# Sums of squares of the gated DeltaNet's queries and keys: two products in fp32r in place of one in float32

## The reference, cut to what matters

```python
def l2norm(x):
    return x * lax.rsqrt(jnp.sum(x * x, -1, keepdims=True) + L2_EPS)

    q = l2norm(c[..., :W_DN].reshape(B, T, H_DN, HEAD_DIM)) * HEAD_DIM ** -0.5
    k = l2norm(c[..., W_DN:2 * W_DN].reshape(B, T, H_DN, HEAD_DIM))
```

## Time and profile before

| | |
|---|---|
| median of three runs | 1552.3 us |
| the profiled execution's own time | 1559.0 us |
| its span | 1557.2 us |
| granted TensorE clock, mean | 0.992 of 2.4 GHz |
| PE busy | 1508.7 us |
| VectorE (DVE) busy | 912.4 us |
| ScalarE (ACT) busy | 651.1 us |
| stage "a" in the trace | about 64 to 375 us |
| DMA over the span | 234 GB/s |

### The profile page before, as it was taken

How to read it: one execution, slowest core, us unless ns; L and a number is a source line. 1 busy time by engine, 2 the same in 40 slices (tenths; PEclk the granted TensorE clock), 3 DMA queues, 4 the chain that set the end, 5 groups by cost and what they waited for, 6 DMA issues and landing times.

```text
span 1557.2 us, 36665 instructions
## 1 busy us (share of the span) xinstructions
PE 1508.7 (97%) x15464; PEld 1458.0 (94%) x15464; DVE 912.4 (59%) x1217; ACT 651.1 (42%) x771; POOL 89.0 (6%) x126
## 2 busy tenths in 40 slices
PE   7999999999889999999999999999999999999996
PEld 7899899999778999997999999999999999999995
DVE  4445646458643466664786666666666644455566
ACT  5344344434425454463643334443333333333344
POOL 0000000002233100001000000000000000000000
PEclk9999999999999999999999999999999999999998
DMA  8788989896678876656555555556767655555453
GB/s 290 262 340 331 338 307 363 304 340 250 248 261 300 311 272 242 217 179 254 190 177 174 171 179 188 169 183 229 251 233 257 208 174 185 189 169 181 162 183 116
DMA packets 72527, 365.11 MB, mean 234 GB/s; under 512 B 9072, under 2 KB 10424, under 8 KB 45656
## 3 DMA queue, kind: packets, MB, share of 16 engines
q1 hardware_dynamic: 56960, 310.00, 56.1%
q0 software_dynamic: 13664, 52.31, 9.1%
q10 hardware_dynamic: 1792, 1.20, 0.3%
HBM read 353.20 MB, written 10.47 MB: 234 GB/s over the span
## 4 chain that ended last, share of the span: by engine, by line
PE 79%; DVE 7%; ACT 4%; DMA 4%; SPq 3%; issue 2%; another core or an unknown queue 1%; POOL 0%; ACTq 0%; DVEq 0%
PE psum_g L538 22%; PE psum_g L539 22%; PE psum_g L540 22%; PE M L2220 3%; DVE wl L522 2%; ACT wh L517 2%; SPq L659 2%; PE M L538 1%; PE M L539 1%; PE M L540 1%; PE psum_g L2560 1%; DMA raw<-w_in_t 1%; DMA sraw<-cache_k_t 1%; PE M L2235 1%
## 5 line engine op out<-in xcount | busy, mean ns | idle before, releaser
L538 PE MATMUL psum_g<-xh,wh 128*128 128x264 f32 (+1 forms) x2382 | 696.5, 292 | 5.9 <-DVE wl L522 3.8
L539 PE MATMUL psum_g<-xl,wh 128*128 128x264 f32 (+1 forms) x2382 | 676.8, 284 | 0.0
L540 PE MATMUL psum_g<-xh,wl 128*128 128x264 f32 (+1 forms) x2382 | 675.9, 284 | 0.0
L522 DVE TENSOR_TENSOR wl<-raw,wh 128x2048 fp32r<-128x2048 f32 (+1 forms) x205 | 461.6, 2252 | 302.4 <-ACT wh L517 301.9
L517 ACT CAST wh<-raw 128x2048 fp32r<-128x2048 f32 (+1 forms) x221 | 414.4, 1875 | 248.2 <-PE psum_g L540 194.4
L538 PEld LDWEIGHTS psum_g<-xh,wh 128*128 128x128 f32 x2382 | 449.4, 189 | 21.7 <-issue 13.3
L539 PEld LDWEIGHTS psum_g<-xl,wh 128*128 128x128 f32 x2382 | 449.8, 189 | 3.2 <-issue 2.9
L540 PEld LDWEIGHTS psum_g<-xh,wl 128*128 128x128 f32 x2382 | 447.9, 188 | 0.0
L538 PE MATMUL psum_g<-gh,wh 128*128 128x264 f32 x704 | 200.3, 285 | 0.2 <-DVE wl L522 0.2
L539 PE MATMUL psum_g<-gl,wh 128*128 128x264 f32 x704 | 199.4, 283 | 0.0
L540 PE MATMUL psum_g<-gh,wl 128*128 128x264 f32 x704 | 199.4, 283 | 0.0
(11 more groups left out here) (474 smaller groups left out, 1693.5 us busy)
## 6 DMA issues: line engine op xcount, KB each, us to landing
raw<-w_t SPq DMA_DIRECT2D x88, 1024.0 KB
raw<-w_in_t SPq DMA_DIRECT2D x53, 1024.0 KB
kring<-cache_k_t SPq DMA_DIRECT2D x96, 512.0 KB, 5.5
sraw<-cache_k_t SPq DMA_DIRECT2D x32, 512.0 KB, 6.5
raw<-w_out_t SPq DMA_DIRECT2D x16, 1024.0 KB
raw<-w2a_t SPq DMA_DIRECT2D x16, 1024.0 KB
raw<-w2b_t SPq DMA_DIRECT2D x16, 1024.0 KB
raw<-w2c_t SPq DMA_DIRECT2D x16, 768.0 KB
```

The lines of the kernel that those rows point to most:

```text
L522: eng.tensor_tensor(wl[:, u % 2, 0:nk], raw[:, u % 2, 0:nk], wh[:, u % 2, 0:nk].bitcast(F32), ALU.subtract).then_inc(raw_used, 1)
L538: nc.tensor.matmul(out, hi_w, x_hi(k), start=(k == order[0]), stop=False)
L539: nc.tensor.matmul(out, hi_w, x_lo(k), start=False, stop=False)
L540: last = nc.tensor.matmul(out, lo_w, x_hi(k), start=False, stop=(k == order[-1]))
```

## The change

1. A tile `sq_r` (2 x 256 columns, fp32r) takes the room of the first slice of `chain`, and `ones_r` is a copy of the ones in fp32r, made once by ScalarE in stage "q". One slice of the nine is given up: the masks (`cm_flat`, `cms`) move from `xi` to `x0`, which `dec` holds until `qkd` is made.
2. ScalarE squares twice: into `rs` as before and, rounded, into `sq_r` (event "hi").
3. PE multiplies `sq_r` by `ones_r` behind product group 10 of unit 4i+5 (`norms_first`, opens the sum in the bank).
4. VectorE, in unit 4i+5 after the convolution and what else stands there and before step 3, waits for that product and replaces `sq_r` by `rs - sq_r` (`squares_low`, event "lo").
5. PE multiplies `sq_r` again at the place of the old product (`norms`, closes the sum), once "lo" is there.
6. VectorE makes the masks in step 5 of the delta rule instead of step 1: one unit later, ahead of the first transpose of the inversion, and after waiting for `qkd`.

```diff
--- before.py
+++ after.py
@@ -190,6 +190,7 @@
         ptab = sb("ptab", [64, PAGES], stack=mix)
         smp = sb("smp", [P, 24, NSAMP], stack=mix)
         g_hc = sb("g_hc", [P, H, 2], stack=mix)
+        ones_r = sb("ones_r", [P, P], F32R, mix)
         picked = sb("picked", [64, TOPK, BLOCKS], stack=mix)
 
 
@@ -233,6 +234,8 @@
 
         kring = sb("kring", [P, K_RING - 2, H, P], stack=mix)
         kring_flat = kring[:].rearrange("p r h t -> p (r h t)")
+        with ExitStack() as shared:
+            sq_r = sb("sq_r", [P, 2, SEQ], F32R, shared)
         chain = sb("chain", [P, 9 * 4 * P + 4 * 2 * P], stack=mix)[:]
 
         def four(index):
@@ -242,7 +245,7 @@
             at = 9 * 4 * P + index * 2 * P
             return chain[:, at:at + 2 * P].rearrange("p (w n) -> p w n", n=P)
 
-        x0, at0, xi, yi, t1, qkd, kd, vb, cm = (four(n) for n in range(9))
+        x0, at0, yi, t1, qkd, kd, vb, cm = (four(n) for n in range(1, 9))
         egb, qd, rk, s1 = (two(n) for n in range(4))
         tg, dec, uu, oc, sf, kcn = x0, x0, x0, x0, egb, rk
 
@@ -252,8 +255,8 @@
         def by32(x):
             return x.rearrange("p (w n) -> p w n", n=32)
 
-        cm_flat = blocks(xi, 0, 4)
-        cms = [by32(blocks(t1, 2))] + [by32(blocks(xi, l)) for l in range(4)]
+        cm_flat = blocks(x0, 0, 4)
+        cms = [by32(blocks(t1, 2))] + [by32(blocks(x0, l)) for l in range(4)]
         atc, t1c = by32(blocks(t1, 0)), by32(blocks(t1, 1))
         t6 = blocks(t1, 2, 2).rearrange("p (w n) -> p w n", n=64)
         xc, yc = by32(blocks(cm, 0)), by32(blocks(cm, 1))
@@ -391,10 +394,11 @@
         s_pool = steps("s_pool", ["ab0", "neg", "relr"])
 
         q_pool, q_dve = (steps(f"q_{e}", [name]) for e, name in (("pool", "clear"), ("dve", "spread")))
-        a_pe = steps("a_pe", ["norm"])
-        a_act = steps("a_act", ["silu_qk", "silu_s", "silu_v", "square", "log", "rsq"])
+        a_pe = steps("a_pe", ["hi", "norm"])
+        a_act = steps("a_act", ["silu_qk", "silu_s", "silu_v", "square", "hi", "log", "rsq"])
         a_dve = steps("a_dve", [f"t{k}{s}" for s in range(3) for k in range(4)] + ["smp"])
         a_nrm = steps("a_nrm", ["q", "k"])
+        a_low = steps("a_low", ["lo"])
         a_pool = steps("a_pool", ["edge"])
         n_act, n_pe, n_dve = (steps(f"n_{e}", names) for e, names in (("act", ["sq", "log", "rsq"]), ("pe", ["sum"]),
                                                                     ("dve", ["q", "k"])))
@@ -405,7 +409,7 @@
         b_pe = steps("b_pe", ["gcb", "kk", "kt", "qk", "vt"] + [f"{n}{l}" for l in lv[1:-1] for n in ("t1_", "xt_")] +
                      [f"{n}{LEVELS - 1}" for n in ("t1_", "xt_")] + ["kc", "u0", "s1", "u1", "s2", "o", "rms"])
         b_act = steps("b_act", ["egb", "dec", "kcn", "u0", "s1", "u1", "sq", "oc", "log", "rsq"])
-        b_dve = steps("b_dve", ["da", "qd", "atc", "at0", "cm0", "cm", "rk", "kd", "qkd", "vb", "ct", "t1_0", "x_0", "y_1"] +
+        b_dve = steps("b_dve", ["da", "qd", "atc", "at0", "rk", "kd", "qkd", "vb", "cm0", "cm", "ct", "t1_0", "x_0", "y_1"] +
                       [n for l in lv[1:-1] for n in (f"t1_{l}", f"x_{l}", f"y_{l + 1}")] +
                       [f"t1_{LEVELS - 1}", "y_end", "sdec", "sf", "ow"])
         b_tg, b_clear = (steps(f"b_{n}", [n]) for n in ("tg", "clear"))
@@ -924,6 +928,8 @@
             nc.scalar.activation(sdec[:].rearrange("p b h -> p (b h)"), M[:, 2, 32:96], ACT.Exp).then_inc(s_act.sem, 1)
             nc.scalar.copy(sbeta[:].rearrange("p b h -> p (b h)"), M[:, 2, 96:160]).then_inc(s_act.sem, 1)
             nc.scalar.copy(beta[:], sigm[:, 0:2].rearrange("p c h -> p h c")).then_inc(s_act.sem, 1)
+            settle(act)
+            nc.scalar.copy(ones_r[:], ones)
             nc.scalar.copy(g_hc[:], gates[:, 0:2].rearrange("p c h -> p h c")).then_inc(s_act.sem, 1)
             act.wait_ge(d_ptab, 16 * NSAMP)
             nc.scalar.copy(ptab[:], ptab_i[:]).then_inc(s_act.sem, 1)
@@ -972,6 +978,7 @@
                 nc.scalar.activation(pj[:, i + 16, 0:SEQ], ct[:, 2, 0:SEQ], ACT.Silu).then_inc(a_act.sem, 1)
                 wait(act, a_act, "silu_qk", i)
                 nc.scalar.activation(rs, cs[:, :, 0:SEQ], ACT.Square).then_inc(a_act.sem, 1)
+                nc.scalar.activation(sq_r[:], cs[:, :, 0:SEQ], ACT.Square).then_inc(a_act.sem, 1)
 
             def norms(i):
                 wait(act, a_pe, "norm", i)
@@ -1428,6 +1435,11 @@
                                                ALU.mult).then_inc(a_nrm.sem, 1)
                 nc.vector.tensor_tensor(head(1, i)[:, 0:SEQ], cs[:, 1, 0:SEQ], rs[:, 1], ALU.mult).then_inc(a_nrm.sem, 1)
 
+            def squares_low(i):
+                wait(dve, a_pe, "hi", i)
+                wait(dve, a_act, "hi", i)
+                nc.vector.tensor_tensor(sq_r[:], rs, sq_r[:].bitcast(F32), ALU.subtract).then_inc(a_low.sem, 1)
+
             def over(row, n=4):
                 return row.unsqueeze(1).to_broadcast([P, n, row.shape[1]])
 
@@ -1474,12 +1486,6 @@
                         ins = nc.vector.tensor_tensor(atc[part(q)], quarter(bank4(B_), q), quarter(dec, q), ALU.mult)
                     vec(ins)
                     vec(nc.vector.tensor_tensor(at0, bank4(B_), dec, ALU.mult))
-                    wait(dve, b_dve, "atc", p)
-                    vec(nc.vector.tensor_tensor(cms[0], atc, over(constant(0)), ALU.mult))
-                    vec(nc.vector.tensor_tensor(cm_flat.rearrange("p (l w n) -> p l w n", l=4, n=32),
-                                                atc.unsqueeze(1).to_broadcast([P, 4, 4, 32]),
-                                                constant(1, 4).rearrange("p (l n) -> p l n", n=32).unsqueeze(2)
-                                                .to_broadcast([P, 4, 4, 32]), ALU.mult))
                 elif s == 2:
                     wait(dve, b_pe, "kt", p)
                     vec(nc.vector.tensor_tensor(rk, odd(bank4(C_)), second(bdec), ALU.mult))
@@ -1493,6 +1499,13 @@
                 elif 5 <= s < 5 + 2 * SMALL:
                     l, xy = divmod(s - 5, 2)
                     if l == 0 and not xy:
+                        wait(dve, b_dve, "atc", p)
+                        vec(nc.vector.tensor_tensor(cms[0], atc, over(constant(0)), ALU.mult))
+                        wait(dve, b_dve, "qkd", p)
+                        vec(nc.vector.tensor_tensor(cm_flat.rearrange("p (l w n) -> p l w n", l=4, n=32),
+                                                    atc.unsqueeze(1).to_broadcast([P, 4, 4, 32]),
+                                                    constant(1, 4).rearrange("p (l n) -> p l n", n=32).unsqueeze(2)
+                                                    .to_broadcast([P, 4, 4, 32]), ALU.mult))
                         wait(dve, b_dve, "cm0", p)
                         vec(nc.vector.transpose(flat4(yc), flat4(cms[0])))
                         wait(dve, b_dve, "ct", p)
@@ -1789,6 +1802,8 @@
                     sample_rows(1)
                 if u > FIRST_Z:
                     gated(u - FIRST_Z - 1)
+                if 1 <= i <= n and c == 1:
+                    squares_low(i - 1)
                 step(3)
                 if 0 <= j < H:
                     scores_max(j)
@@ -2225,8 +2240,12 @@
                             last.then_inc(k_used, 1)
 
             def norms(i):
-                wait(pe, a_act, "square", i)
-                nc.tensor.matmul(M[:, D_], ones, rs.rearrange("p s n -> p (s n)"), start=True, stop=True).then_inc(a_pe.sem, 1)
+                wait(pe, a_low, "lo", i)
+                nc.tensor.matmul(M[:, D_], ones_r[:], sq_r[:].rearrange("p s n -> p (s n)"), start=False, stop=True).then_inc(a_pe.sem, 1)
+
+            def norms_first(i):
+                wait(pe, a_act, "hi", i)
+                nc.tensor.matmul(M[:, D_], ones_r[:], sq_r[:].rearrange("p s n -> p (s n)"), start=True, stop=False).then_inc(a_pe.sem, 1)
 
             def delta(p, s):
 
@@ -2402,6 +2421,8 @@
                     head_turn(j - 1)
                 elif k == 6 and 0 <= j - 1 < H:
                     head_values(j - 1)
+                if k == 10 and 0 <= u // 4 - 1 < n and u % 4 == 1:
+                    norms_first(u // 4 - 1)
                 if k == 1:
                     if u == KEY_UNITS + 1:
                         wait(pe, se_act, "rows0")
```

## The result

Measured beside the kernel before, the changed kernel took 1566.3 us (median of 8) against 1553.1: an estimated ratio of 1.0073, 95% interval 1.0055 to 1.0092 (the two medians alone would give 1.0085). Two later measurements of the same kernel gave 1.0046 (1.0028 to 1.0063) and 1.0048 (1.0030 to 1.0067). The mean of the three, 1.0056, is +8.7 us. The forecast was +3.6 with a range up to +6.7: the sign was right, and the forecast was less than half of what was measured.

A forecast was written before the change was run, and what follows sets the result against it. TensorE, busy for 97% of the span, was taken to bound the kernel. Up to unit 33 +3.0, chain to 411 +0.1, clock -1.2 and +1.7 gave +3.6 on 1552.3: 1555.9 us, range 1552.3 to 1559.0.

The forecast's parts named there:

- Where the stalls stand and how long they are: PE idles for VectorE's remainder behind units 5, 9 and 33: 2.3, 2.1, 2.9 us; no wait at heads 2 to 6.
- The saving per head: At each norm, two fp32r products (0.47) replace one float32 product (0.86): 0.39 us saved, 3.1 at most for eight.
- I take one fall of three: +1.7: Behind the three new stalls, each costing between nothing and 1.7 us of clock, one clock fall was counted.
- the fall at 411 "avoided", -1.2: PE's idle before 411 shrinks from 3.65 to 1.4 us, so the half-speed clock at 412 does not happen: -1.2.
- Head 7 "off the path": Behind unit 33 PE is 2.5 us late, but off the path because PE waits 3.65 us at 411 anyway.
- The moved masks: Mask products one unit later: free for the first three pairs; at the last pair, steps before L1492 come 0.65 us earlier.
- The rival of two and three falls: More than one clock fall behind the stalls: two +5.3, three +7.0 us; chance with the forecast's one fall, 0.53.
- The Trainium skill's rule: Only longer idle gaps than these stalls lower the clock; this is the no-fall rival, +1.9 us, 1554.2, chance 0.33.
- The in-time rival: Remainder ready before PE arrives at the norms: -2.1 us, 1550.2; with page loads keeping up, -3.4, 1548.9; chance 0.12.

The follow-up runs named there:

- after_again: The changed kernel itself, unchanged, measured and profiled a second time beside the kernel before: ratio 1.0046 to the kernel before.
- wait_only: Changed kernel with the old float32 product back and no short-format products; second Square, remainder and the wait for it stay: 1.0069 to the kernel before, +10.7 us.
- early_7: Changed kernel, last head only: first product two groups earlier, remainder ahead of the nine gather steps; first two heads' stalls stay: 1.0046 to the kernel before, +7.2 us.
- early_01: Changed kernel, first two heads only: first product four groups earlier, remainder ahead of lower weights; last head's stall stays: 1.0029 to the kernel before, +4.5 us.
- filled_01: Changed kernel with 16 unread products of 264 columns run by TensorE in place of idling at the first two heads' stalls: 1.0040 to the kernel before, +6.2 us.
- pool_low8: Changed kernel with all eight remainders on GpSimd, first product behind group 5 (last head: group 8): 1.0012 to the kernel before.

## Why the prediction was wrong in size

- **Where the stalls stand and how long they are**: right. Forecast 2.3, 2.1, 2.9; measured 2.28, 2.28, 2.75. None at heads 2 to 6. But the forecast counted from where the next product could have started, the view from the end of the last one's record; counted as the forecast did, the first two are 2.44 each, 0.15 and 0.3 more than forecast, and "lo" behind them costs 0.33 (in after_again) where the forecast took 0.28. By the starts of the units TensorE was 2.2 later each, not 1.9 and 1.8: +0.7 on the sum.
- **The saving per head**: right. Where nothing disturbs, TensorE gains 0.40 per head from unit to unit (mended heads 0 and 1, over units 5 and 6 and over 9 and 10); forecast 0.39. Over seven heads it is the 2.7 above.
- **The failed step is in the part on the clock: "I take one fall of three: +1.7."** Over all profiles with these stalls (three of the change, wait_only, early_7, early_01, filled_01's last) 13 of 16 were followed by a clock of 0.50; the three that were not had 2.28, 2.29 and 2.75 of idle. A fall costs 1.5 behind the first two, a little under the 1.7 taken. Three stalls at 13 in 16 are 3 x 0.81 x 1.5 = 3.7 in place of 1.7. The mechanism was right, the number of falls was not.
- **Its neighbour, the fall at 411 "avoided", -1.2**, was right in its mechanism and too large. In all six profiles in which TensorE waited 3.3 to 3.7 us for L1661 (or its line in the variant) a fall followed; in none of the eleven with 1.4 to 2.0. But in eight of those eleven a fall came a few microseconds earlier, at the end of the sixteen small products of L2479 or right behind them (two of the three profiles of the change among them). Behind the small products or behind the wait, three of the six profiles with the last head's stall have a fall, and all eleven without it. So about half of the 1.2 may be taken off, 0.6. The trace of before shows the small products too, 399.06 to 402.15, with full clock behind them, so this was not to be read from it. A second point hides here: without the stall the wait for L1661 is 3.3 to 3.7 if no fall comes before it and 1.74 to 2.01 if one does, so such a fall costs next to nothing, it uses up a wait. With the stall the wait is 1.44 or 1.45 in all six, fall or not: what ends it is then behind TensorE's own work (the "qk" product), so there the fall is on the path. The 1.4 itself was luck in part: the forecast's own terms, 3.65 + 0.1 - 2.5, give 1.25.
- **Head 7 "off the path"**: half right. Without a fall it cost under 1 us; with falls behind it 1 to 5.
- **The moved masks**: no cost was seen, as forecast; the gain of 0.65 was not seen either, though intervals of 2 us could hide both. In three profiles with the masks moved the wait for L1661 is 3.34 or 3.35, against 3.65 and 3.67 before, but 3.65 in pool_low8 too: at most 0.3 of it is there.
- Put together: the forecast's 3.6 without its two steps of the clock (-1.2, +1.7) is 3.1; with 0.7 for the longer stalls, 3.7 for three likely falls and -0.6 at 411 it is 6.9, against 8.7 measured (1.0028 to 1.0092 over the three intervals). This is an estimate from the profiles; what the remaining 1.8 is, no run tells.
- **The rival of two and three falls** (1557.6 and 1559.3) was the case that came: three in the first profile of the change, two in each of the others. It was held to be less likely than one fall. The reason given against (one stretch with 1.56 idle that kept the clock) said nothing of stalls of 2.3, and the range left three falls out.
- **The Trainium skill's rule** ("TensorE: Matmul & The Clock Gate", HAM oscillation), by which gaps as short as these leave the clock alone, does not hold here: 2.28 was followed by 0.50 in the rows above.
- **The in-time rival** named a gain of 2.1. Two ways to make the remainder timely gave +1.1 and +1.2 us (means). That is some 3 us short of it, with intervals of up to 3 us on either side of each measurement. The saving is in the profiles (the 2.7 above), so something else takes it. More waits for pages (4.1 to 6.0 us in the four mended profiles, 1.6 and 1.7 with only the masks moved) are a possible taker, but the two profiles of the kernel before had 1.0 and 7.8. This stays open.

## What to carry to other kernels

A wait put into an engine that is never idle costs its length and, on TensorE, what the clock loses behind it: two stalls of 2.3 us here, with falls of 1.5 behind most of them, came to more than twice what eight savings of 0.4 could bring in. Before splitting a product in two halves, one of which needs another engine, place that engine's step by its queue, not by its duration: 0.69 us of work was ready 6.6 us after its input (107.3 to 113.9). And where all engines work in order, a late result holds up what stands behind its reader (here the next weights' cast), so sending only the second half later mended a part (+3.1 in place of +8.7); doing the remainder earlier mended nearly all (+1.1). And a saving of 3 us in all is no more than what this kernel's waits vary by from one execution to the next: look for it in the distance of starts, not in the total alone.

## What was not expected of the hardware

- Products that keep TensorE busy by the profile's count can be followed by a fall like an idle engine: sixteen small products in 3.09 us, with no wait in them, had one at their end or right behind them in eight of seventeen profiles.
- A fall goes with the length of TensorE's wait and not with what it waits for: none behind 33 waits of 1 to 1.5 us, 26 behind 30 of 2.07 to 3.68.
- The same stall, to 0.01 us, is followed by a fall of the clock in one execution and not in the next: 2.28 at the first head with 0.50 behind it in one profile and 1.00 in another.
- Small products in the inversion (32x32) sometimes stand still for 1.1 to 2.4 us with nothing that they wait for in the profile (the line "issue" above), near 180 us in eight of the profiles, in or after windows in which the DMA share was near 1 (1.05 from 178 to 180 in the first profile of the change). Which resource they lack, no run tells.
- The kernel before itself differs by 8 us between sessions (1554.6 against 1562.2), as does the stretch from 405 to 472 in the profiles (57 against 65), whichever variant it is.
